# Gates of the first head on ScalarE, low parts of its shifted inputs on VectorE, in a hybrid retention and HGRN2 layer

## The reference, cut to what matters

```python
h = rms_norm(x, norm_w)
h = h * (1.0 + scale[:, None, :]) + shift[:, None, :]
proj = h @ w_in
rq, rk, rv, rg, hq, hf_f, hf_b, hi, hg = jnp.split(proj, N_IN_PARTS, axis=-1)

def forget(z, lb):
    f = lb[None, None, :] + (1.0 - lb[None, None, :]) * jax.nn.sigmoid(z.astype(F32))
    return heads(jnp.log(f), HG_HEADS), heads(1.0 - f, HG_HEADS)

lf_f, k_f = forget(hf_f, hg_lb[0])
lf_b, k_b = forget(hf_b, hg_lb[1])
```

## Time and profile before

| | us |
|---|---|
| median of 3 runs | 1449.74 |
| lowest and highest run | 1449.27, 1450.53 |
| the profiled execution's own time | 1449.74 |
| its span in the trace | 1447.8 |
| mean granted clock of PE in it | 0.996 of full |
| busy: PE, DVE, ACT, POOL | 1425.8, 985.0, 496.4, 389.5 |

### The profile page before, as it was taken

The page is one execution under the profiler, slowest core; times in us unless marked ns, Lnnn a source line. Parts: engine busy times, 40 slices in busy tenths (PEclk is TensorE's granted clock), DMA queues, the critical chain, the costliest instruction groups (busy, mean ns, idle before and its releaser), DMA issues.

```text
span 1447.8 us, 28169 instructions
## 1 busy us (share of the span) xinstructions
PE 1425.8 (98%) x11545; PEld 1284.7 (89%) x11545; DVE 985.0 (68%) x1296; ACT 496.4 (34%) x866; POOL 389.5 (27%) x308
## 2 busy tenths in 40 slices
PE   7999999999999999999999999999999999999997
PEld 6998799989998999899989998999899988788886
DVE  5734995666888788878887788667566758632345
ACT  4322443233332333243234323332343234321234
POOL 0001562511341134114411431143114315301220
PEclk9999999999999999999999999999999999999998
DMA  9998222314342434343433333232223247173235
GB/s 379 377 362 345 91 90 79 95 59 142 115 132 90 135 110 126 104 129 109 130 99 123 118 123 107 68 96 74 96 66 100 70 146 257 56 263 130 88 102 203
DMA packets 69310, 202.06 MB, mean 140 GB/s; under 512 B 7872, under 2 KB 16336, under 8 KB 63440
## 3 DMA queue, kind: packets, MB, share of 16 engines
q1 hardware_dynamic: 69168, 200.39, 40.6%
q10 hardware_dynamic: 32, 0.02, 0.0%
HBM read 179.65 MB, written 16.53 MB: 136 GB/s over the span
## 4 chain that ended last, share of the span: by engine, by line
PE 94%; DVE 2%; DMA 2%; POOL 1%; ACT 1%; issue 0%; SPq 0%; DVEq 0%; ACTq 0%
PE ps L1955 36%; PE ps L1984 10%; PE ps L1986 10%; PE ps L1985 10%; PE ps L2160 5%; PE ps L2162 5%; PE ps L2161 5%; PE ps L1841 3%; PE ps L2003 2%; PE ps L1816 2%; DMA area<-in_w_mod 1%; PE ps L2014 1%; PE ps L2025 1%; PE ps L2054 0%; PE ps L2097 0%
## 5 line engine op out<-in xcount | busy, mean ns | idle before, releaser
L1113 DVE TENSOR_TENSOR w_lo<-area,w_hi 128x1024 fp32r<-128x1024 f32 x144 | 193.0, 1340 | 267.1 <-ACT w_hi L653 266.6
L653 ACT ACTIVATE w_hi<-area 128x1024 fp32r<-128x1024 f32 x144 | 152.4, 1058 | 561.0 <-PE ps L1955 271.6
L1955 PE MATMUL ps<-hT_hi,w_hi 128*128 128x320 f32 x1184 | 274.6, 313 | 0.0
L1955 PE MATMUL ps<-hT_hi,w_lo 128*128 128x320 f32 x1184 | 269.7, 309 | 0.0
L1955 PE MATMUL ps<-hT_lo,w_hi 128*128 128x320 f32 x1184 | 269.7, 309 | 0.0
L1984 PE MATMUL ps<-w_hi,hT_hi 128*128 128x512 f32 x640 | 253.3, 396 | 3.2 <-DVE w_lo L1113 3.2
L1986 PE MATMUL ps<-w_hi,hT_lo 128*128 128x512 f32 x640 | 250.0, 391 | 0.0
L1985 PE MATMUL ps<-w_lo,hT_hi 128*128 128x512 f32 x640 | 249.8, 390 | 0.0
L1955 PEld LDWEIGHTS ps<-hT_hi,w_hi 128*128 128x128 f32 x1184 | 196.4, 188 | 2.7 <-issue 1.6
L1955 PEld LDWEIGHTS ps<-hT_lo,w_hi 128*128 128x128 f32 x1184 | 197.9, 188 | 0.0
L1955 PEld LDWEIGHTS ps<-hT_hi,w_lo 128*128 128x128 f32 x1184 | 197.9, 188 | 0.0
(11 more groups left out here) (268 smaller groups left out, 2026.9 us busy)
## 6 DMA issues: line engine op xcount, KB each, us to landing
area<-in_w_in SPq DMA_DIRECT2D x144, 512.0 KB, 3.7
area<-in_w_mod SPq DMA_DIRECT2D x32, 1024.0 KB, 9.3
area<-in_w_out SPq DMA_DIRECT2D x38, 512.0 KB, 3.8
gate_raw<-in_w_gate SPq DMA_DIRECT2D x32, 512.0 KB, 3.8
area<-in_x_columns SPq DMA_DIRECT2D x4, 1280.0 KB, 9.8
area<-in_w_first SPq DMA_DIRECT2D x5, 1024.0 KB, 7.7
o_hi_scratch<-area SPq DMA_DIRECT2D x14, 320.0 KB, 2.2
o_lo_scratch<-area SPq DMA_DIRECT2D x14, 320.0 KB, 2.6
```

What stands on the lines that cost most here:

```text
L653: act.activation(w_hi[:, n % 2, :], raw[:, n % 3, :], ACT.Copy).then_inc(wt_hi.sem, 1)
L1113: v.tensor_tensor(w_lo[:, n % 2, :], raw[:, n % 3, :], w_hi[:, n % 2, :].bitcast(F32), ALU.subtract).then_inc(wt_lo.sem, 1)
L1955: ins = mm(out[s], wt[:, n % 2, w], x[:, k, s * HALF:(s + 1) * HALF], start=k == 0 and step == 0, stop=k == KT - 1 and step == 2)
```

## The change

In the first head alone, ACT makes the gates and their complements (`first_gates`, four activations of the function Identity with a scale and a bias, 128 x 640 each, at the end of stage 12 in its queue), and DVE no longer does. Also, DVE makes the low parts of the shifted slices, in pairs: inputs k and k+1, then low parts k and k+1. POOL no longer does. The other heads keep DVE's gates.

```diff
--- before.py
+++ after.py
@@ -714,6 +714,16 @@
                         i = act.activation(buf[:, tokens], buf[:, tokens], ACT.Identity, bias=corr[:, part_, w:w + 1])
                 i.then_inc(r_fixed.sem, 1)
 
+            def first_gates(h):
+
+                act.wait_ge(h_gate.sem, h_gate.at(h, 6))
+                for s in range(2):
+                    col = slice(s * HEADS + h, s * HEADS + h + 1)
+                    act.activation(KL[:, s, :], KL[:, s, :], ACT.Identity, scale=oml[:, col], bias=lb[:, col]).then_inc(h_gate.sem, 1)
+                act.wait_ge(h_gate.sem, h_gate.at(h, 8))
+                for s in range(2):
+                    act.activation(K[:, s, :], KL[:, s, :], ACT.Identity, scale=-1.0, bias=ones[:, 0:1]).then_inc(h_gate.sem, 1)
+
             def projected(h, i):
                 act.wait_ge(wt_used.sem, wt_used.at(h, UNITS - 1 if first_head(h) and i == 0 else UNITS if first_head(h) and i == 1 else 2 * i + 2))
 
@@ -887,6 +897,8 @@
                 if prev is None:
                     for k in shifted_slices(n):
                         high_shifted(k)
+                if n == 12 and prev is None:
+                    first_gates(h)
                 if n == 11 and prev is not None:
                     act.wait_ge(h_q.sem, h_q.at(h))
                     if due(lq, h - 1):
@@ -1219,10 +1231,18 @@
                                                op0=ALU.add, op1=ALU.add)
                 i.then_inc(s_mod.sem, 1)
 
+            def low_shifted(k):
+
+                dve.wait_ge(s_hi.sem, s_hi.at(k))
+                v.tensor_tensor(hT_lo[:, k, :], shifting[k % 2], hT_hi[:, k, :].bitcast(F32), ALU.subtract).then_inc(s_lo.sem, 1)
+
             def shifted(ks):
 
-                for k in ks:
+                for k in ks[::2]:
                     shifted_input(k)
+                    shifted_input(k + 1)
+                    low_shifted(k)
+                    low_shifted(k + 1)
 
             def correction_rows():
 
@@ -1464,7 +1484,7 @@
                     dve.wait_ge(h_gate.sem, h_gate.at(h, at + 1))
                     reciprocal_half(buf, 0, h_gate)
                     reciprocal_half(buf, 1, h_gate)
-                if n == 12:
+                if n == 12 and prev is not None:
 
                     dve.wait_ge(h_gate.sem, h_gate.at(h, 6))
                     for s in range(2):
@@ -1475,6 +1495,7 @@
                         dve.wait_ge(la.sem, la.at(h - 1))
                     for s in range(2):
                         v.tensor_scalar(K[:, s, :], KL[:, s, :], -1.0, 1.0, ALU.mult, ALU.add).then_inc(h_gate.sem, 1)
+                if n == 12:
 
                     tmp = sT[:, 0:REL]
                     if prev is None:
@@ -1729,14 +1750,7 @@
                     pool.wait_ge(pe_level.sem, pe_level.at(h - 1))
                 g.tensor_tensor(XE[:, 1, 1, :], K[:, 0, :], K[:, 1, :], ALU.add).then_inc(la.sem, 1)
 
-            def low_shifted(k):
-                pool.wait_ge(s_hi.sem, s_hi.at(k))
-                g.tensor_tensor(hT_lo[:, k, :], shifting[k % 2], hT_hi[:, k, :].bitcast(F32), ALU.subtract).then_inc(s_lo.sem, 1)
-
             def items(n, h, prev):
-                if prev is None:
-                    for k in shifted_slices(n):
-                        low_shifted(k)
                 if prev is not None:
                     if n == 0:
                         key_factors(prev)
```

## The result

| | before | after |
|---|---|---|
| median of 7 runs each | 1449.74 us | 1454.12 us |
| lowest and highest | 1449.27, 1451.13 | 1453.55, 1454.35 |
| the profiled run, and its span | 1449.74, 1447.8 | 1454.10, 1452.3 |

The changed kernel is slower by 4.4 us between the two medians. The ratio over all runs is 1.0026 with a 95% interval of 1.0017 to 1.0035, which is 3.8 us. The forecast was 1455.0 in a range of 1450.0 to 1458.0.

A forecast was written before the change was run, and what follows sets the result against it. PE, busy 98% of the span, was taken as the bound. Chunk 15 late by 5.1 us plus 0.4 at chunk 16 made 5.5, reduced to +5.3 on 1449.74: 1455.0 us, range 1450.0 to 1458.0.

The forecast's parts named there:

- The new wait in stage 10: DVE waits for ACT's hT_hi(4) until 147.28; w_lo(12), which PE wanted at 152.30, would end alone at 154.6.
- The terms set at nothing: Stage 9's low parts (3.3 us if uncovered), chunk 17 and SP's later loads (4 us if uncovered) cost nothing.
- POOL's moved work: POOL's cosine products start at 153.05 instead of 164.07, meet w_lo(12) and hold DVE up, 2.7 us.
- the 6.63 us of DVE time: Stage 12: two gate lines of four instructions, 3.70 + 2.93 us, leave DVE.
- The wait ahead of chunk 13: PE waits 3.7 us for w_lo(13), ready at 166.3; a half-clock stretch in chunk 12 would be hidden in it.
- The gates on ACT: Gates at 0.93 and complements at 0.8 us, 3.2 in all, precede w_hi(14); PE waits 1.3 ahead of chunk 14.
- The meeting at w_lo(15): POOL's query products, starting early at 180.55, meet w_lo(15), which ends near 182.95; PE waits 1.6 ahead of chunk 15.
- The 4.9 us of the stall: PE's old wait ahead of chunk 14, 3.2 us, plus 1.7 for the half-clock stretch in that chunk.
- rival 2: The stall simply goes, if w_lo(12) is there by 152.30 and w_lo(13) by 159.15: 1444.8 us; chance 0.06.
- Rival 1: POOL and DVE do not block each other at the ports: +1.5 us, 1451.2, as little as -0.4; chance 0.24.
- Rival 3: A half-clock stretch that no wait hides, 1.7 us each: 1456.7 us, with two 1458.4; chance 0.15.
- Rival 4: The change does nothing here because DVE's order hides all: 1449.7 us; chance 0.05.

The follow-up runs named there:

- late_low: The changed kernel, but in stage 10 DVE makes low parts 4 and 5 after the first gate's reciprocals; 1450.81 us.
- low_only: The changed kernel with the gates of all heads on DVE again, low parts still on DVE; 1453.35 us.
- cosine_later: The changed kernel, but POOL's two cosine products of the first head wait for the second gate's add, to run beside its reciprocals; 1452.21 us.
- gates_only_behind: The kernel before, but with the first head's gates on ACT behind w_hi(14); POOL keeps the low parts; 1449.26 us.

## Why the prediction was right, step by step

**The new wait in stage 10** was the step that decided, and it held: DVE idle 3.49, low parts from 147.54 (forecast 147.28, plus the 0.3 that this run was late), late_low gives its price, 3.3 us. The terms set at nothing held too: none of PE's waits on w_lo falls into stage 9 or ahead of chunk 17, and from the second head on PE waits as before.

**POOL's moved work** held in kind. The cosine products cost 1.00 in w_lo(12) and 1.02 in the inputs behind it, 2.0, where I had taken 2.7. Most of the difference is that each takes POOL 1.3 alone; the 1.53 of the row that I used was lengthened by DVE's gates beside it. The same meeting lengthened the gates, so the 6.63 us of DVE time that the prediction counts as removed are only 2.0 where POOL is quiet (low_only). cosine_later measures 1.9 for it. The wait ahead of chunk 12 came out at 3.13 (forecast 3.45).

**The wait ahead of chunk 13** was forecast as 3.7 with a half-clock stretch hidden in it. It was 1.56, and chunk 12 lasted 166.08 - 1.56 - 155.89 = 8.63 us instead of 6.85, so the stretch of 1.8 was there and was absorbed. Together they are 3.3, and chunk 13 started at 166.08 where I had 166.35.

**The gates on ACT** held best: forecast 0.93 and 0.8, measured 0.91 and 0.82, w_lo(14) 8.1 us after the pair began as in the working (8.2). The Trainium skill gives 93 ns for each operand read per partition (ScalarE: Activation LUTs, "What ACT_TABLE_LOAD costs"), and the trace is near it: 0.91 against 0.74 for two of them and 0.82 for one, 0.08 to 0.09 each. The wait ahead of chunk 14 was 0.93 (forecast 1.3).

**The meeting at w_lo(15)** is a term that was mis-sized. I had POOL's query products start first and hold w_lo(15) for 1.3. DVE's w_lo(15) started at 180.21 and POOL's product at 180.23, so DVE went first, w_lo(15) took its bare 1.22, and chunk 15 waited 0.25 instead of 1.6. The blocking fell on the next group instead, 5.33 for 1.93, which is 3.4 where I had 2.8. Chunk 16 waited 0.62 (0.4). Chunk 15 was 3.6 late where I had 5.1, and chunk 16 4.6 where I had 5.5. Chunk 16 is 0.9 us less late than the working had it. Of this, about 0.5 is this term (1.1 less ahead of chunk 15, 0.6 more behind it), about 0.6 are the shorter cosine products and 0.15 the gates on ACT, less the 0.3 that this run was late already. That the forecast of +5.3 lies only 0.9 from the measured 4.4 owes a little to that 0.3. The Trainium skill describes an exclusive lock where the order of issue decides who blocks (SBUF — State Buffer, "Who interferes with whom"). Both places fit it: at w_lo(12) POOL was first by 0.12 us and DVE was held up, at w_lo(15) DVE was first by 0.02 and POOL was.

**The 4.9 us of the stall**, which rival 2 takes as its price, was counted too high. The stretch's 1.7 in it was almost all hidden by w_lo(15), as shown in the section on the result.

**Rival 1** (the ports do not bite) fell with cosine_later. **Rival 2** (the stall simply goes) needed w_lo(12) by 152.30 and got it at 155.84. **Rival 3** did not happen: the one stretch fell where a wait absorbed it. **Rival 4** fell, as every run of the changed kernel is slower than every run of the kernel before beside it.

## What to carry to other kernels

Before moving work onto an engine, ask what its in-order list will wait for at that spot and what is queued behind it: the same change cost 4.4 us with the instructions of three engines in one order and saved 4.0 with them in another. An engine that is relieved starts its next work earlier, so look up what that will meet. Put GpSimd's work beside VectorE instructions that do not contend with it, here the reciprocals.

## What was not expected of the hardware

A half-clock stretch did not follow the length of a wait in any plain way. Such stretches came after waits of 3.19 us in the kernel before and 3.13 in the changed one, but also after waits of 2.07 (cosine_later, ahead of chunk 13) and 2.28 (gates_only_behind), and none came after a wait of 2.06 in cosine_later (ahead of chunk 12) or after the two waits of 3.12 and 3.07 in low_only, where the granted clock was 1.00 throughout from 150 to 185 us. The two waits of cosine_later:

```profile
154.79 0.50 PE L1999 MATMUL ps<-w_hi,hT_hi 128*128 128x512 f32 x1 [2.06 <-DVE w_lo L1125]
...
163.95 0.78 PE L1999 MATMUL ps<-w_hi,hT_hi 128*128 128x512 f32 x1 [2.07 <-DVE w_lo L1125]
```

What decides it stays open. What a stretch costs depends on when the next low parts are done, and not only on whether PE waits behind it. In the changed kernel a wait absorbs it. In late_low and cosine_later chunk 13 took 8.5 us and no wait follows, but w_lo(15) was done only 0.05 us before chunk 15 started (178.26 and 178.31 in late_low), so the 1.7 us are not lost there either. In gates_only_behind w_lo(16) was done at 182.29 for a chunk that started at 186.73, and there the stretch costs its 1.7 us in full. And 0.02 us decided which of DVE and POOL was held up at w_lo(15).
